# Weight halves at their own byte offsets to the activations, 128 and 256 modulo 512

## Time and profile before

| | us |
|---|---|
| median of 3 executions (2163.43 to 2165.67) | 2164.01 |
| the profiled execution | 2162.32 |
| its span, first to last instruction | 2160.5 |
| TensorE, matmuls | busy 2095.5 (97%) |
| TensorE, weight loads | busy 1697.5 (79%) |
| VectorE | busy 1146.3 (53%) |
| ScalarE | busy 816.6 (38%) |
| GpSimd | busy 38.4 (2%) |
| mean DMA rate | 88 GB/s |

### The profile page before, as it was taken

One profiled execution on the slowest core, in us unless ns is written; L12 is line 12 of the kernel. 1 busy time (PEld: TensorE's weight loads), 2 busy tenths in 40 slices (PEclk: granted clock), 3 DMA queues, 4 the chain that ended last, 5 costly groups with the idle time before them and its releaser, 6 DMA issues. The chain is left out here.

```text
span 2160.5 us, 26090 instructions
## 1 busy us (share of the span) xinstructions
PE 2095.5 (97%) x10710; PEld 1697.5 (79%) x10710; DVE 1146.3 (53%) x1706; ACT 816.6 (38%) x1169; POOL 38.4 (2%) x34
## 2 busy tenths in 40 slices
PE   8999999999999999999999999999999899999998
PEld 6876678888888887787878888887786577888886
DVE  5674765542542579888846444324634736444423
ACT  4324753331232465542534222213325734322212
POOL 0120000000000000000100000000000000000000
PEclk9999999999999999999999999999999999999999
DMA  4220012223223222233122222222240031222221
GB/s 177 86 83 35 2 59 99 94 95 109 85 96 103 91 81 100 108 117 97 40 98 74 95 95 94 95 96 95 98 173 23 1 118 59 98 98 98 98 98 68
DMA packets 43111, 190.68 MB, mean 88 GB/s; under 512 B 15520, under 2 KB 16224, under 8 KB 22384
## 3 DMA queue, kind: packets, MB, share of 16 engines
q1 hardware_dynamic: 40656, 184.78, 25.0%
q10 hardware_dynamic: 2336, 4.23, 0.6%
HBM read 185.25 MB, written 3.74 MB: 87 GB/s over the span
## 5 line engine op out<-in xcount | busy, mean ns | idle before, releaser
L250 DVE TENSOR_TENSOR weights_low<-weights_raw,weights_high 128x2048 fp32r<-128x2048 f32 (+1 forms) x161 | 365.8, 2272 | 565.4 <-ACT weights_high L223 565.3
L441 PE MATMUL psum<-split,weights_high 128*128 128x512 f32 x1448 | 568.3, 392 | 8.3 <-PEq L146 4.2
L442 PE MATMUL psum<-split,weights_high 128*128 128x512 f32 x1448 | 564.6, 390 | 0.0
L443 PE MATMUL psum<-split,weights_low 128*128 128x512 f32 x1448 | 564.6, 390 | 0.0
L223 ACT CAST weights_high<-weights_raw 128x2048 fp32r<-128x2048 f32 (+1 forms) x161 | 304.0, 1888 | 545.3 <-PE psum L443 504.7
L441 PEld LDWEIGHTS psum<-split,weights_high 128*128 128x128 f32 x1448 | 272.2, 188 | 70.3 <-issue 8.4
L443 PEld LDWEIGHTS psum<-split,weights_low 128*128 128x128 f32 x1448 | 272.0, 188 | 57.4
L442 PEld LDWEIGHTS psum<-split,weights_high 128*128 128x128 f32 x1448 | 272.0, 188 | 56.0
L443 PE MATMUL psum<-hidden_high,weights_low 128*128 128x512 f32 x256 | 99.6, 389 | 0.0
L441 PE MATMUL psum<-hidden_high,weights_high 128*128 128x512 f32 x256 | 99.6, 389 | 0.0
L442 PE MATMUL psum<-hidden_low,weights_high 128*128 128x512 f32 x256 | 99.6, 389 | 0.0
(11 more groups left out here) (485 smaller groups left out, 3081.4 us busy)
## 6 DMA issues: line engine op xcount, KB each, us to landing
weights_raw<-in_weights SPq DMA_DIRECT2D x161, 1024.0 KB, 4.9
minus_c<-minus_c_rows ACTq DMA_DIRECT2D x16, 256.0 KB, 7.3
x_stream<-in_x SPq DMA_DIRECT2D x4, 512.0 KB, 7.1
gdn_in_grown<-gdn_rows SPq DMA_DIRECT2D x4, 512.0 KB, 4.7
chain_grown<-gdn_rows SPq DMA_DIRECT2D x4, 512.0 KB, 3.7
out<-end_results SPq DMA_DIRECT2D x8, 256.0 KB, 2.1
table<-rope_tables SPq DMA_DIRECT2D x1, 1024.0 KB, 12.0
weights_raw<-in_weights SPq DMA_DIRECT2D x1, 768.0 KB, 4.2
```

Of the source, the lines that this page charges most:

```text
L250: self.nc.vector.tensor_tensor(out=self.low_of(n)[:, 0:width], in0=self.raw[:, n % 2, 0:width], in1=self.high_of(n)[:, 0:width].bitcast(se ...
L441: nc.tensor.matmul(bank, wh, ah, start=first, stop=False)
L442: nc.tensor.matmul(bank, wh, al, start=False, stop=False)
L443: return nc.tensor.matmul(bank, wl, ah, start=False, stop=last)
```

## The change

`weights_high` and `weights_low` become one tensor `weights_halves` of 4 x 2048 + 64 columns. In it stand high of slot 0, low of slot 0, high of slot 1, low of slot 1. Those of slot 0 begin 32 columns (128 bytes) later than a multiple of 8192 bytes, those of slot 1 begin 64 columns (256 bytes) later. `arena_offset` grows from 40 to 104 columns, from 160 to 416 bytes. With the 256 bytes of the longer tensor, everything behind it moves by 512 bytes: the activations keep their place modulo 512 to `weights_raw`, and `const`, `gains` and `conv` move by 256. No instruction is added or taken away, and shapes, types, waits and order stay.

```diff
+SLOT_OFFSETS = (32, 64)
...
-        self.high = enter(nc.sbuf_tensor("weights_high", [P, 2, CHUNK], f32r))
-        self.low = enter(nc.sbuf_tensor("weights_low", [P, 2, CHUNK], f32r))
+        halves = enter(nc.sbuf_tensor("weights_halves", [P, 4 * CHUNK + SLOT_OFFSETS[1]], f32r))
+        self.high, self.low = [[halves[:, at + n * CHUNK:at + (n + 1) * CHUNK] for n, at in zip((first, first + 2), SLOT_OFFSETS)]
+                               for first in range(2)]
...
     def high_of(self, n):
-        return self.apart[n][0] if n in self.apart else self.high[:, n % 2, :]
+        return self.apart[n][0] if n in self.apart else self.high[n % 2]
 
     def low_of(self, n):
-        return self.apart[n][1] if n in self.apart else self.low[:, n % 2, :]
+        return self.apart[n][1] if n in self.apart else self.low[n % 2]
...
-        self.nc.gpsimd.tensor_tensor(out=self.low[:, chunk.slot, 0:width],
+        self.nc.gpsimd.tensor_tensor(out=self.low[chunk.slot][:, 0:width],
                                      in0=self.raw[:, chunk.slot, 0:width],
-                                     in1=self.high[:, chunk.slot, 0:width].bitcast(self.f32),
+                                     in1=self.high[chunk.slot][:, 0:width].bitcast(self.f32),
                                      op=self.sub).then_inc(self.low_ready, 1)
...
-        enter(nc.sbuf_tensor("arena_offset", [P, 40], f32))
+        enter(nc.sbuf_tensor("arena_offset", [P, 104], f32))
```

## The result

The changed kernel takes 2183.3 us (median of 4 executions, 2181.6 to 2184.9) against 2163.7 us (4 executions of the kernel before, 2162.2 to 2165.7): 1.009 times the time before, 95% interval 1.0072 to 1.0107. Its profiled execution is 2182.8 us with a span of 2181.0 us, 20.5 us longer than before. It is slower, where no change was forecast.

A forecast was written before the change was run, and what follows sets the result against it. TensorE's matmul pace, 226.7 ns, was taken to bound the kernel. Span 2160.5 plus 1.8 us around it plus zero gave 2162.3 us, profiled 1.7 us under the median, so 2164.0 us was forecast; range 2158 to 2183 us.

The forecast's parts named there:

- What bounds the kernel: TensorE, busy 97% of the span: matmuls follow every 226.7 ns, 7,788 of them making 1,766 us.
- Part 1, +256: Odd slot's weight halves at +256 bytes to the activations: pace stays as before, effect zero.
- Part 1, +128: Even slot's weight halves at +128 bytes to the activations: effect zero, between bounds of -52 and +18 us.
- the upper bound for the even slot: Even slot's 3,890 matmuls at the 16-column product's 231.3 ns instead of 226.7 ns: +18 us.
- the two figures that price everything: TensorE's matmul stream: 13.4 ns paid per matmul above pure streaming, and 231 to 233 ns out of step after breaks.
- The even slot never in step: Rival: all the even slot's matmuls run at 231.3 ns, +18 us, 2182 us; chance 8%.
- Falling out of step at each chunk: Rival: each of 163 offset changes between chunks costs 46 ns, +7.5 us, 2171.5 us; chance 14%.
- +128 freeing the read: Rival: the even slot's matmuls run at 213.3 ns, -52 us, 2112 us; chance 9%.
- 13.4 ns to be had: TensorE's matmuls: the pace of 226.7 ns less an assumed pure streaming time of 213.3 ns.
- Parts 2 and 3: ScalarE's copy and VectorE's subtraction on the halves, and constants moved 256 bytes against the activations: zero each.
- A reader of weights and one of activations that get in each other's way: In TensorE, interference by address that would explain both the 13.4 ns per matmul and the out-of-step 231 to 233 ns.
- the spells out of step: After every break the matmul stream runs at 231 to 233 ns before it falls into 226.7 ns.

## Why the prediction was wrong, point by point

- **What bounds the kernel** held: the pace of the matmuls did it, and nothing else moved. PE's share is 97% as before.
- **Part 1, +256: right.** The earlier trace rows showed exactly this case, 128 columns at 256, and the run with only that slot moved has a ratio of 1.0005. The small cost of entering is one interval of 231 ns at each change.
- **Part 1, +128: the step that failed.** The text took zero "because the earlier trace rows stand on either side of 128 in kind (wide load, constant offset) and both give 226.5 ns". That was an interpolation between two points of a quantity that isn't smooth: 4 bytes beside a good place cost as much as 128. And one of the points was not what it was taken for: the 80 columns of the earlier trace rows don't speak for 128 columns. At 192 these have 229.0 or 233.3 ns where those were in step, and 80 columns from 0, where 128 columns are in step, have 233.3 ns. What stood in the place of zero: 232.4 against 226.7 ns at +128, about 21 us.
- **The earlier trace rows were put aside** as a matter of short loads or of a changing offset. Their 231.3 ns gave the upper bound for the even slot, 3,890 x 4.6 = +18 us, 2182 us. Why those 16-column loads are slow wasn't tested; that their bound came near is partly luck. A better price stood in the earlier trace rows, which the text itself names as one of the two figures that price everything: out of step the stream ran at 232 and 232.5 ns. That is 3,890 x 5.6 = 22 us, about 2186 us. Measured were 5.7 ns, and about 21 us in even chunks (the 3,890 also count 96 matmuls of the two even chunks kept apart).
- **The rivals.** The even slot never in step (8%) is what happened. Falling out of step at each chunk (14%) didn't: the odd slot loses under 1 us in all, and with a constant +128 the loss doubled instead of going away. +128 freeing the read (9%) was wrong in sign. Of its premise, 13.4 ns to be had, the run with a still stream shows 10.9 ns, but no run shows that an address frees any of it.
- **Parts 2 and 3: right**, zero each (1885 and 2271 ns; the constants moved in the run with ratio 1.0005).
- **The range**, up to 2183 us, ended at the size of that rival, with 4.6 ns where 5.7 were measured, and misses the median of 2183.3 us by a hair. A bound taken from a far row needed room beyond its own number.
- **A reader of weights and one of activations that get in each other's way** was the text's own guess at what the 13.4 ns and the spells out of step have in common, and it got no share in the zero for +128. By an offset alone the runs have 2203.3 us against 2164.1 us, and with the stream still or moving 215.8 ns against 226.7 and 232.4 ns.

## What stays open

What decides the pace of a narrow load, and why one place has two paces (229.1 and 233.3 ns at 448 and 192, 226.5 and 233.3 ns at 16, 232.4 and 233.3 ns at 128, 226.7 and 231 ns for the same 80 columns), wasn't settled. That the two readers get in each other's way fits most of the runs, but no run shows where they would meet, or why the costs go by 256 bytes. How much of the 10.9 ns between a still and a moving stream belongs to the loads is open. A load that runs in the opposite direction, a moving stream without loads, and one with a still stream in a correct product weren't tried.

## What to carry to other kernels

In a stream of 512-column float32r matmuls with a weight load for each, place the loaded and the streamed operand at a multiple of 256 bytes to each other; anything else that was measured cost on average 1.5 to 7.5 ns of 227 per matmul in the MLP, and up to 11 ns where the weights stream: with both slots off, 1.3 to 2.3% of this kernel. Look for it in start-to-start times by chunk, as busy time and mean duration hardly show it (2116.8 against 2095.5 us, 395 against 392 ns). And where a parameter has no row of its own, neighbours on both sides are no bound unless something shows that the quantity is smooth.

## What the runs showed of the hardware

- The pace depends on the relation of two SBUF addresses modulo 256 bytes, though weight load and stream belong to one engine: 226.7 ns at 0 and 256, 232.2 ns with the loaded operand 4 bytes above, 236.5 ns and more with it 4 bytes below.
- Off that place the pace isn't a function of the offset alone: 128 columns at +16 ran at 233.3 ns in most chunks and in step, 226.5 ns, in three that followed a break, and at 192 at 229 or 233.3 ns.
- The width of the load counts beside its place: at 128, 80 columns had 228.1 and 128 columns 232.4 ns.
- With the streamed operand on one column the pace is 215.8 ns at either offset; with it moving, the best is 226.7 ns. With the loaded operand on one column and the stream moving it is 231.0 to 231.7 ns, at either offset.
- At +128 the intervals of the MLP's chunks repeat in a cycle of seven matmuls: 241, 232, 231, 232, 228, 230, 233 ns, each to 1 ns, and begin again, 232.4 ns on average.
- In the run with partial loads a weight load takes 134 ns for 64 columns, 148 for 80, 161 for 96 and 188 for 128.
- What the type of the operands is worth in the kernel before: in step, matmuls of 512 float32r columns follow at 226.7 ns. Those of 512 float32 columns in the latent attention (`k_a`, `q_a`, 96 rows) follow at (204.01 - 203.15)/2 us, 430 ns:

```profile
203.15 0.59 PE L876 MATMUL psum<-k_a,q_a 96*128 96x512 f32 x1
...
204.01 0.59 PE L876 MATMUL psum<-k_a,q_a 96*128 96x512 f32 x1
```
